# A hybrid decoder step on one core: the rotary embedding's swapped halves by DMA instead of by a TensorE product

## What is computed

```python
def rotary(x, positions):
    half = x.shape[-1] // 2
    ...
    x1, x2 = jnp.split(f32(x), 2, axis=-1)
    return jnp.concatenate([x1 * cos - x2 * sin, x2 * cos + x1 * sin], axis=-1).astype(x.dtype)
...
    h = rms_norm(x, mix_norm)
    proj = h @ w_in
    ...
    q = rotary(rms_norm(q, q_norm), positions)
    k = rotary(rms_norm(k, k_norm), positions)
```

## Time and profile before

| | us |
|---|---|
| median of 3 runs | 2339.82 |
| the profiled execution, its own time | 2340.49 |
| its span in the profile | 2338.7 |
| TensorE matmuls busy | 2328.7 (100%) |
| VectorE busy | 1458.8 (62%) |
| ScalarE busy | 984.2 (42%) |

### The profile page before, as it was taken

How to read it: one execution, slowest core, us unless ns; L and a number is a source line. 1 busy time by engine, 2 the same in 40 slices (tenths; PEclk the granted TensorE clock), 3 DMA queues, 4 the chain that set the end, 5 groups by cost and what they waited for, 6 DMA issues and landing times.

```text
span 2338.7 us, 57551 instructions
## 1 busy us (share of the span) xinstructions
PE 2328.7 (100%) x23152; PEld 2301.0 (98%) x23152; DVE 1458.8 (62%) x2007; ACT 984.2 (42%) x1268; POOL 87.8 (4%) x146
## 2 busy tenths in 40 slices
PE   9999999999999999999999999999999999999999
PEld 8999999999999999999999999999999999999999
DVE  7555455555556668878676767766555555545554
ACT  6333333333334544665332446544333333333333
POOL 0000000000002100000000000120000000000000
PEclk9999999999999999999999999999999999999999
DMA  7666567555555656545333637655555555555555
GB/s 242 203 227 212 180 216 246 182 184 181 180 173 173 228 192 203 164 138 185 105 105 114 225 123 216 218 180 180 179 180 185 177 182 183 181 181 182 183 165 172
DMA packets 124082, 428.27 MB, mean 183 GB/s; under 512 B 14488, under 2 KB 20760, under 8 KB 123424
## 3 DMA queue, kind: packets, MB, share of 16 engines
q1 hardware_dynamic: 117504, 393.49, 51.3%
q0 software_dynamic: 6432, 32.64, 4.3%
HBM read 415.21 MB, written 21.33 MB: 187 GB/s over the span
## 4 chain that ended last, share of the span: by engine, by line
PE 95%; DMA 2%; DVE 1%; ACT 1%; issue 0%; DVEq 0%; SPq 0%; ACTq 0%
PE bank L272 30%; PE bank L273 30%; PE bank L274 29%; PE bank L1266 3%; DMA raw<-in_weights 1%; DVE wlo L245 1%; ACT whi L239 0%; DMA x<-in_x 0%; PE bank L1404 0%; PE bank L1308 0%; PE bank L1619 0%; PE bank L1397 0%; PE bank L1483 0%; DVE sq L323 0%; PE bank L1380 0%
## 5 line engine op out<-in xcount | busy, mean ns | idle before, releaser
L245 DVE TENSOR_TENSOR wlo<-raw,whi 128x1024 fp32r<-128x1024 f32 (+3 forms) x794 | 913.4, 1154 | 603.3 <-ACT whi L239 601.0
L272 PE MATMUL bank<-hhi,whi 128*128 128x264 f32 x4048 | 1164.0, 288 | 2.7 <-DVE wlo L245 2.7
L239 ACT ACTIVATE whi<-raw 128x1024 fp32r<-128x1024 f32 (+3 forms) x794 | 792.4, 1001 | 874.8 <-PE bank L274 850.0
L273 PE MATMUL bank<-hlo,whi 128*128 128x264 f32 x4048 | 1147.3, 283 | 0.0
L274 PE MATMUL bank<-hhi,wlo 128*128 128x264 f32 x4048 | 1146.0, 283 | 0.0
L272 PEld LDWEIGHTS bank<-hhi,whi 128*128 128x128 f32 x4048 | 762.4, 188 | 11.9 <-issue 3.8
L273 PEld LDWEIGHTS bank<-hlo,whi 128*128 128x128 f32 x4048 | 762.9, 188 | 1.2
L274 PEld LDWEIGHTS bank<-hhi,wlo 128*128 128x128 f32 x4048 | 759.1, 188 | 0.0
L272 PE MATMUL bank<-mhi,whi 128*128 128x264 f32 x1408 | 399.5, 284 | 0.0
L274 PE MATMUL bank<-mhi,wlo 128*128 128x264 f32 x1408 | 398.9, 283 | 0.0
L273 PE MATMUL bank<-mlo,whi 128*128 128x264 f32 x1408 | 398.9, 283 | 0.0
(11 more groups left out here) (275 smaller groups left out, 1672.6 us busy)
## 6 DMA issues: line engine op xcount, KB each, us to landing
raw<-in_weights SPq DMA_DIRECT2D x666, 512.0 KB, 3.3
raw<-in_weights SPq DMA_DIRECT2D x64, 384.0 KB, 3.1
out_skv<-in_cache POOLq DMA_DIRECT2D x16, 512.0 KB, 3.8
raw<-in_weights SPq DMA_DIRECT2D x32, 256.0 KB, 3.5
raw<-in_weights SPq DMA_DIRECT2D x32, 192.0 KB, 2.4
side<-stg POOLq DMA_DIRECT2D x18, 132.0 KB, 3.7
gates<-side POOLq DMA_DIRECT2D x1, 2376.0 KB, 13.4
x<-in_x SPq DMA_DIRECT2D x4, 528.0 KB, 6.5
```

Source lines behind the costliest of these rows:

```text
L239: act.activation(whi[:, u % RING, 0:n], raw[:, u % RING, 0:n], ACT.Copy).then_inc(hi_done, 1)
L245: dve.tensor_tensor(wlo[:, s, 0:n], raw[:, s, 0:n], whi[:, s, 0:n].bitcast(F32), ALU.subtract).then_inc(lo_done, 1)
L272: pe.matmul(bank[:, 0:T], hi, xhi[:, k], start=(k == 0), stop=False)
L273: pe.matmul(bank[:, 0:T], hi, xlo[:, k], start=False, stop=False)
```

## The change

Four DMAs a tile, issued by ScalarE, copy the 32-partition quarters of `qkv[:, t]` into `qs[:, t % 2]` with each pair of quarters exchanged; the sign is put into the table of sines; VectorE multiplies `qs` in place. The permutation, the 12 products with it and their semaphores are gone. ScalarE's new step `turn(t)` stands in iteration t + 7 behind the first split, and waits for `q_nrm` of tile t and for `q_add` of tile t - 2. VectorE's `rotated(t)` keeps its place and waits for 64 counts of `q_turned[t % 2]`.

```diff
@@ constants @@
-    rot = np.zeros((P, P))
-    for m in range(P):
-        if m % HD < HD // 2:
-            rot[m + HD // 2, m] = -1.0
-        else:
-            rot[m - HD // 2, m] = 1.0
-    c["rot"] = rot
...
-    c["cos"], c["sin"] = np.cos(ang), np.sin(ang)
+    c["cos"], c["sin"] = np.cos(ang), np.where(d[:, None] % HD < HD // 2, -np.sin(ang), np.sin(ang))
@@ mix_act @@
             for n in range(3 * AT):
                 hi("qkv", n, 0)
+                if n >= 7:
+                    turn(n - 7)
...
             for m in range(3 * RT):
                 hi("rkv", m, 0)
+                if m == 0:
+                    turn(2 * AT - 1)
...
+        def turn(t):
+
+            act.wait_ge(q_nrm, t + 1)
+            if t >= 2:
+                act.wait_ge(q_add, t - 1)
+            for q in range(4):
+                act.dma_start(qs[32 * q:32 * q + 32, t % 2], qkv[32 * (q ^ 1):32 * (q ^ 1) + 32, t]
+                              ).then_inc(q_turned[t % 2], 16)
@@ rotated @@
-            dve.wait_ge(q_rot, t + 1)
-            dve.tensor_tensor(qs[:, t % 2], cossin[:, 1], A4[2 + t % 2][:, 0:T], ALU.mult).then_inc(q_sin, 1)
+            dve.wait_ge(q_turned[t % 2], 64 * (t // 2 + 1))
+            dve.tensor_tensor(qs[:, t % 2], cossin[:, 1], qs[:, t % 2], ALU.mult)
@@ mix_pe @@
-                if n >= 7:
-                    rotate(n - 7)
...
-                if m == 0:
-                    rotate(2 * AT - 1)
-                elif m == 2:
+                if m == 2:
                     new_rows()
...
-        def rotate(t):
-            pe.wait_ge(q_nrm, t + 1)
-            if t >= 2:
-                pe.wait_ge(q_sin, t - 1)
-            pe.matmul(A4[2 + t % 2][:, 0:T], cc("rot"), qkv[:, t], start=True, stop=True).then_inc(q_rot, 1)
```

More of the change, by code:

```diff
@@ L560, in build @@
             "pre_done", "shift_a", "shift_v", "lora_act", "lora_pe", "lora_out"))
-        q_sq, q_ss, q_root, q_nrm, q_rot, q_sin, q_add = map(sem, (
-            "q_sq", "q_ss", "q_root", "q_nrm", "q_rot", "q_sin", "q_add"))
+        q_sq, q_ss, q_root, q_nrm, q_add = map(sem, ("q_sq", "q_ss", "q_root", "q_nrm", "q_add"))
+        q_turned = [sem("q_turned0"), sem("q_turned1")]
         u_pe, u_act, u_vec, key_in = sem("u_pe"), sem("u_act"), sem("u_vec"), sem("key_in")
```

## The result

The changed kernel takes 2348.89 us (median of 7 runs, 2346.85 to 2350.86); the kernel before took 2340.48 on the same occasion (7 runs, 2339.52 to 2343.95). The ratio is 1.0036 with an interval of 1.0026 to 1.0045: **8.4 us slower**, where 5.3 us faster was forecast, and above the range's end of 2340.6. The profiled execution of the changed kernel took 2348.11 us, its span is 2346.3; the one before had 2340.49 and 2338.7, so the two profiles differ by 7.6 us.

What follows compares the result with a forecast made beforehand. TensorE was taken to bound the kernel; ten products at 0.44 and two at 0.45 us sum to 5.3 us off the median 2339.82, with nothing lost elsewhere: 2334.5 us. Whole range 2333.9 to 2340.6.

Steps and rivals of the forecast that it cites:

- What leaves TensorE: Ends of blocks 7 to 17 and first `rkv` block: removing 12 products saves TensorE 10 x 0.44 + 2 x 0.45 = 5.3 us.
- What ScalarE gets: ScalarE in `turn`: 48 DMA issues, four a tile, taken at 0.38 us each including the gap, 1.5 us a tile.
- x: Time ScalarE spends issuing one tile's four DMAs between its two splits; forecast 1.5 us.
- The high end of the bounds, 0.72: Price of one ScalarE DMA issue if it equals SP's longest, 0.72 us; kept for the rivals and the range.
- some 0.1 us a tile: ScalarE's issues: waiting up to 0.33 us now and then if SP's and ScalarE's sequencers can't issue at once.
- Who waits behind it: Behind ScalarE's DMAs: square, second split, VectorE's split, inversion and scaling, then the next `turn`; nothing lost at x = 1.5.
- The ring: Cycle between ScalarE and VectorE in the `qkv` loop, 4.97 + x a round; 6.47 us against TensorE's 6.24.
- The lead: From VectorE finishing a second split to the start of TensorE's block needing it; 18.6 - 11x left, 2.1 us forecast.
- 11x - 18.6: TensorE's loss in us once the lead is used up, beyond x = 1.69.
- Rival 2: ScalarE held longer an issue, by contention with SP or slower issuing; at 0.72 us 2347.6 us; slower had chance 0.12.
- Costs at nothing: Landing may take 6.4 us before `rotated` needs the copies; VectorE's work unchanged within 0.02; squares come early enough.
- The rival from the Trainium skill: ScalarE's issues cost 0.43 us whatever their size, x = 1.9, 2336.8 us; part or no gain had chance 0.42.

Runs made afterwards that it cites:

- e1: Changed kernel without the exchange of halves: no DMA, no permutation product, qs filled with zeros; 2335.62 us, 4.6 less than before.
- e7: Changed kernel with the same four DMAs a tile issued by SP between its weight loads instead of by ScalarE; 2335.68 us, 4.0 less than before.
- e12: Changed kernel with four ScalarE copies a tile in place of the DMAs, moved behind the second split and the root; 2335.13 us, 4.5 less than before.
- e9: Changed kernel with one straight DMA of 128 partitions a tile instead of four, halves not exchanged; 2336.59 us, 3.1 less than before.
- e10: Changed kernel with the four DMAs a tile reading rows of input x in HBM instead of qkv; 2342.36 us, 2.7 more than before.
- e2: Changed kernel with the same four ScalarE DMAs a tile moved behind the second split and the root; 2337.06 us, 3.2 less than before.
- e4: Changed kernel with four ScalarE copies of 32 partitions in place of the four DMAs, at the same place; 2336.98 us, 3.3 less than before.

## Why the prediction was wrong

- **"What leaves TensorE"**: right. 5.3 us were forecast, and 5.19 are gone from the stretch (e1). The forecast time of 2334.5 is within 1.2 us of what e1, e7 and e12 take. The half block of 3.35 us in the earlier trace rows is the first `rkv` block's and not block 17's; the prediction uses it rightly.
- **"What ScalarE gets"**: this step failed, "I take 0.38 ... and x = 4p = 1.5". With its gap of 0.03 an issue took 0.64 in a row, and a tile 2.44. Two things were taken wrongly. The rise in a row, which the rows showed (0.48), was set aside for "a quarter of the rows to describe"; e9 and e10 show that fewer rows are no cheaper. And all the nearest rows were of transfers to or from HBM; e10 shows that a source in SBUF is dearer, 0.61 against 0.44. The high end of the bounds, 0.72, did take the price in, but got the small chance of 0.12. One reason was that SP's 28 issues of that stretch cost 0.333; those stand alone, and these in a row of four.
- **"some 0.1 us a tile"** for two sequencers that can't issue at once: wrong in size and in reason. The second issue of five of the first eleven bursts was clearly longer than 0.61, by 2.9 us together, 0.27 a tile, and that was not SP's doing: SP's load runs beside ScalarE's third issue and lengthens neither (last section). Without these five the loss would be 11 x 2.44 - 17.7 = 9.1, and the kernel still 3.9 slower; so the price of the issue decides the sign, and the long issues add the rest.
- **"Who waits behind it"**: right in form. The ring is there; its fixed part is 5.05 (forecast 4.97; the difference is ScalarE's restart, 0.10 from the last DMA's issue at 856.67 to the square at 856.77, which the prediction named and left out of the sum). The lead is used up in block 12, and the loss follows the bursts. 11x - 18.6 with x = 29.8/11 gives 11.2 against 12.04 measured. From the 2.1 us of spare lead that the forecast had, the price takes 10.3 (11 x 0.94), the long issues 2.9, the fixed part 0.9: 12.0 lost.
- **Rival 2** named the outcome, slower by dear issues, and had too small a chance. Of its two reasons slower issuing is borne out and contention with SP is not. Its 2347.6 for 0.72 an issue is close to the 2348.89 in part by luck: an issue cost 0.64, the rest came from the long ones.
- **"Costs at nothing"**: the landing (3.5 median) was as allowed for; its longest, 7.7, is over the 6.4 allowed and held VectorE once, for 0.6 us. VectorE's work a block is the 6.03 of before.
- The rival from the Trainium skill, page "DMA: Bandwidth & Descriptors", section "Why a DMA increments its semaphore by 16 and not by 1" (512 sequencer cycles a copy instruction, by the prediction's estimate 0.43 us), was nearer than my choice but still low: 0.61 here in a row, 0.47 for one full tile. It would have given x = 1.9, where the threshold is 17.7/11 = 1.61. The trace doesn't agree with a price that is the same for every copy.
- What stays open: the ring and the product explain 6.85 of the 8.4 us. Another 0.75 of the profiles' difference lies ahead of and behind the stretch, and the changed kernel's profiled execution is 0.8 under its median.

## What to carry to other kernels

Price a DMA issue as work of the engine that issues it, at the price in a row and for the same kind of source and destination. Here no row was of that kind, and the sum with the highest bound came nearest. Then look at what is queued behind the issues: the same issues cost 12 us inside a ring of two engines, 0.9 behind the step that the other engine waits for, and nothing on SP's queue. And if ScalarE has the time, small copies of its own can be cheaper than issuing DMAs for them: here 1.72 us for four against 2.45.

## What the runs showed of the hardware

- Issuing a copy of 32 x 264 from SBUF to SBUF took 0.61 us on ScalarE in a row (0.51 as the first), 0.59 on SP and 0.50 on GpSimd; with a source in HBM 0.44 on ScalarE (0.32 as the first); one copy of 128 x 264 within SBUF 0.47; SP's loads of weights, alone, 0.333.
- ScalarE issued DMAs beside its own running activation, and ahead of one that stands before them in the program, where their semaphores had been met (e2).
- Some issues took 0.85 to 1.59 us. Single issues of one burst of the changed kernel, and SP's in it:

```profile
861.72 0.51 ACTq L858 DMA_DIRECT2D qs<-qkv  x1
862.26 1.59 ACTq L858 DMA_DIRECT2D qs<-qkv  x1
```

```profile
863.00 0.33 SPq L1640 DMA_DIRECT2D raw<-in_weights  x1
```

SP's load is not what holds them up. In all twelve bursts it starts 1.28 to 1.30 us after the first issue. The long one is the second issue in all five cases, and at its usual 0.61 it would have been over by then. In an ordinary burst the load falls beside the third issue, and neither takes longer:

```profile
854.22 0.51 ACTq L858 DMA_DIRECT2D qs<-qkv  x1
855.41 0.61 ACTq L858 DMA_DIRECT2D qs<-qkv  x1
```

```profile
855.50 0.33 SPq L1640 DMA_DIRECT2D raw<-in_weights  x1
```

What the long issues go with is in the trace's DMA packets. The page has a queue of the kind "instruction", by its name the loading of program code (packets, MB, share):

```profile
q8 instruction: 115, 1.88, 0.3%
```

Its packets have 16 KB and take 0.88 us or more. Each of the five long issues overlaps one of them, and ends 0.37 to 0.39 us after that packet does (the one from 862.26 to 863.85: its packet ends at 863.47). All runs with these DMAs from ScalarE or SP together have 25 issues that are over 0.2 us longer than the median and overlap such a packet; all 25 end 0.34 to 0.39 us after it. One more, 0.74 us in e10, overlaps none. One of the 25 is SP's own issue of 1.29 us in e7, where ScalarE issues nothing. Not every packet holds an issue: the first of a burst kept its time in the changed kernel, and of its 45 loads by SP that met one 43 stayed under 0.36 us. So the long issues follow the loading of code, by 25 coincidences and no experiment; how the one holds the other stays open.

- ScalarE copies 32 partitions to another 32 in 0.42 us, 264 elements each, and four such in 1.72 (e4).
